# A two-layer decoder with a mixture-of-experts block: the order of the first loads, norms and projections

## The reference, cut to what matters

```python
mem_n = rms_norm(mem, mem_norm_g)               # 256 memory rows of 1024
h = rms_norm(x, g_mix_pre[0])                   # 512 tokens of 1024
proj = h @ w_in[0]                              # 1024 -> 1408 columns
q, k, v, qm = ...                               # 12 query heads, 3 key heads, 3 value heads, 4 memory-query heads
tok = mixer_a(q, k, v, attn_sink[0], cos_p, sin_p)   # rotary, banded attention of radius 128, with a sink
mkv = mem_n @ w_mem_kv[0]                       # 1024 -> 512: memory keys and values
mo = memory_attention(qm, km, vm)
o = jnp.concatenate([tok, mo], axis=-1) @ w_o[0]
```

## Time and profile before

| what | us |
|---|---|
| median of 3 runs | 2366.46 |
| lowest and highest run | 2361.76 and 2366.80 |
| the profiled execution, its own time | 2361.32 |
| its span | 2359.4 |
| PE busy in the span | 2047.8 (87%) |
| DVE busy | 1086.5 (46%) |
| ACT busy | 615.6 (26%) |

### The profile page before, as it was taken

One profiled execution on the slowest core, in us unless ns is written; L12 is line 12 of the kernel. 1 busy time (PEld: TensorE's weight loads), 2 busy tenths in 40 slices (PEclk: granted clock), 3 DMA queues, 4 the chain that ended last, 5 costly groups with the idle time before them and its releaser, 6 DMA issues. The chain is left out here.

```text
span 2359.4 us, 28557 instructions
## 1 busy us (share of the span) xinstructions
PE 2047.8 (87%) x11901; PEld 1430.9 (61%) x11901; DVE 1086.5 (46%) x2065; ACT 615.6 (26%) x1154; POOL 82.3 (3%) x103
## 2 busy tenths in 40 slices
PE   4977999999999899999999798878778999667772
PEld 2455478888864564788888686666455667322231
DVE  2058554446345774654463665563355344311113
ACT  1025322223121562322231333331143121000001
POOL 0000000000000000000000001110000000000001
PEclk8999999999999999999999898999889999688896
DMA  6120033232131200332331430000101235699994
GB/s 229 36 72 1 1 107 107 72 107 107 63 134 38 78 1 1 108 107 78 101 107 63 146 122 22 3 3 23 62 27 36 81 112 183 241 390 395 397 397 164
DMA packets 146770, 266.80 MB, mean 113 GB/s; under 512 B 6695, under 2 KB 69390, under 8 KB 146446
## 3 DMA queue, kind: packets, MB, share of 16 engines
q1 hardware_dynamic: 140302, 241.85, 29.3%
q0 software_dynamic: 3456, 12.58, 1.5%
q10 hardware_dynamic: 2880, 10.49, 1.1%
HBM read 250.22 MB, written 18.87 MB: 114 GB/s over the span
## 5 line engine op out<-in xcount | busy, mean ns | idle before, releaser
L237 PE MATMUL ps<-arena 64*64 64x64 f32 (+10 forms) x6136 | 870.9, 363 | 154.2 <-DMA arena<-in_moe_w_gu 55.1
L237 PEld LDWEIGHTS ps<-arena 64*64 64x64 f32 (+2 forms) x6136 | 461.3, 155 | 534.2 <-issue 392.0
L247 PE MATMUL ps<-arena 128*128 128x128 f32 (+2 forms) x1181 | 178.5, 301 | 95.5 <-DVE arena L354 27.8
L247 PEld LDWEIGHTS ps<-arena 128*128 128x128 f32 (+2 forms) x1181 | 144.4, 153 | 148.0 <-issue 65.7
L377 DVE TENSOR_SCALAR arena<-arena 128x1024 int32<-128x1024 int32 (+1 forms) x204 | 138.0, 677 | 144.1 <-PE ps L243 83.6
L241 PE MATMUL ps<-HTr,WH1r 128*128 128x512 f32 (+1 forms) x448 | 170.1, 380 | 1.2 <-ACT T16r L956 1.2
L241 PE MATMUL ps<-HTr,WH0r 128*128 128x512 f32 (+1 forms) x448 | 169.8, 379 | 1.2 <-ACT T16r L956 1.2
L384 ACT ACTIVATE WH0r<-arena 128x1024 fp32r<-128x1024 f32 x86 | 91.5, 1063 | 215.8 <-DVE slot2r L380 92.3
L243 PE MATMUL ps<-T16r,WH0r 128*128 128x512 f32 (+1 forms) x384 | 144.1, 375 | 0.0
L243 PE MATMUL ps<-T16r,WH1r 128*128 128x512 f32 (+1 forms) x384 | 143.9, 375 | 0.0
L384 ACT ACTIVATE WH1r<-arena 128x1024 fp32r<-128x1024 f32 x82 | 87.2, 1064 | 198.4 <-DVE slot0r L380 106.2
(11 more groups left out here) (363 smaller groups left out, 2834.5 us busy)
## 6 DMA issues: line engine op xcount, KB each, us to landing
arena<-in_moe_w_gu SPq DMA_DIRECT2D x32, 2048.0 KB, 18.4
arena<-in_w_gate_up SPq DMA_DIRECT2D x44, 1024.0 KB, 6.8
arena<-in_moe_w_down SPq DMA_DIRECT2D x32, 1024.0 KB, 14.7
arena<-in_w_down SPq DMA_DIRECT2D x8, 2048.0 KB, 7.8
arena<-in_w_in SPq DMA_DIRECT2D x7, 2048.0 KB, 11.1
arena<-in_w_in SPq DMA_DIRECT2D x9, 1024.0 KB, 5.4
arena<-in_w_o SPq DMA_DIRECT2D x4, 2048.0 KB, 7.8
y_scr<-arena ACTq DMA_DIRECT2D x16, 512.0 KB, 6.8
```

The lines of the kernel that those rows point to most:

```text
L237: return e.matmul(o, l, r, start=start, stop=stop, skip_group_check=True)
L247: return e.transpose(o, i, ident[0:n, 0:n])
```

## The change

SP's list begins with the four token tiles, each with a semaphore of its own, then the 128 columns of the constants that hold the identity, and the first two norm weights. Behind them stand the first chunk of columns, the memory rows, the memory's weights, the second chunk, the third chunk (now into T16), and last the rest of the constants, the other 15 norm weights and the small tables. PE transposes only the first 16 rows of GR at first; the whole table is transposed behind the last bank.

The norm of the token tiles comes first, and DVE scales tile i + 1 before it moves tile i out. PE makes the first chunk's bank for tile i as soon as that tile is out, with the transposes of tiles 2 and 3 between the banks. The memory's transposes stand between the first and the second chunk, its first bank between the second and the third, the first two quarters of its keys between banks of the third chunk, its second bank behind it, and the last two quarters in the attention, at the places of layer 1. The memory rows move to the region PB and the scratch of the token norm to XSC, so that T16 is free for weights.

```diff
...
-        d_const, d_mem, d_gain, d_x, d_small = [mark(n, queue, 16) for n in (
-            "const_in", "mem_in", "gains_in", "x_in", "small_in")]
+        d_const, d_mem, d_gain, d_small, d_first = [mark(n, queue, 16) for n in (
+            "const_in", "mem_in", "gains_in", "small_in", "ident_in")]
+        d_x = [mark(f"x{i}_in", queue, 16) for i in range(NT)]
...
-        T16J = QKVJ(1, 2)
+        T16J = [QKVJ(l, 2) for l in range(2)]
...
         def load(e, j):
-            if j == T16J:
-                e.wait_ge(*a_post["dn", 0, "x", 3])
+            if j in T16J:
+                if j == T16J[1]:
+                    e.wait_ge(*a_post["dn", 0, "x", 3])
                 e.dma_start(jobs[j][0][0](T16f), jobs[j][0][1]).then_inc(*d_t16.up(j))
                 return
...
+        MEMI, XSC = i4(PBf), i4(place("XSC", U0 + 9728, 4096))
         NORMS = dict(
-            mem=(lambda i: T16[:, i], 2, 1024, lambda i: T16[:, 2 + i], gcol("mem_norm_g"), MEMT),
-            x=(lambda i: X[:, i], 4, 1024, lambda i: T16[:, i], gcol("g_mix_pre", 0), HT),
+            mem=(lambda i: MEMI[:, i], 2, 1024, lambda i: MEMI[:, 2 + i], gcol("mem_norm_g"), MEMT),
+            x=(lambda i: X[:, i], 4, 1024, lambda i: XSC[:, i], gcol("g_mix_pre", 0), HT),
...
-        def v_norm_tile(e, tag, i):
+        def v_norm_scaled(e, tag, i):
             src, nt, D_, scr, g, dst = NORMS[tag]
             ms, rs = [a[:, i:i + 1] for a in NS[tag]]
             e.wait_ge(*a_norm[tag, i])
             e.tensor_scalar(ms, ms, eps6, None, ALU.add).then_inc(*v_norm.up(tag, "ms", i))
             e.wait_ge(*g_pow[tag, i])
             e.tensor_scalar(scr(i), src(i), rs, None, ALU.mult).then_inc(*v_norm.up(tag, "h", i))
+
+        def v_norm_turned(e, tag, i):
+            src, nt, D_, scr, g, dst = NORMS[tag]
             for k0 in range(0, D_ // P, 4):
                 n = min(4, D_ // P - k0)
                 iv = k4(held(tag, i, k0)[:, 0:n * P])
                 e.wait_ge(*p_norm[tag, i, k0])
                 e.tensor_tensor(dst[:, k0:k0 + n, i * P:(i + 1) * P], iv, g[:, k0:k0 + n].unsqueeze(2).broadcast_to((P, n, P)),
                                 ALU.mult).then_inc(*v_norm.up(tag, "out", i, k0))
+
+        def v_norm_tile(e, tag, i):
+            v_norm_scaled(e, tag, i)
+            v_norm_turned(e, tag, i)
+
+        def v_norm_tiles(e, tag):
+
+            for i in range(NORMS[tag][1] + 1):
+                if i < NORMS[tag][1]:
+                    v_norm_scaled(e, tag, i)
+                if i:
+                    v_norm_turned(e, tag, i - 1)
...
         def p_qkv_first(e):
-            for c in range(3):
-                loaded(e, QKVJ(0, c))
+
+            p_norm_tile(e, "x", 0)
+            p_norm_tile(e, "x", 1)
+            loaded(e, QKVJ(0, 0))
+            for i in range(NT):
+                e.wait_ge(*v_norm["x", "out", i, 4])
+                p_qkv_bank(e, 0, i, 0)
+                if i < 2:
+                    p_norm_tile(e, "x", i + 2)
+            for i in range(2):
+                p_norm_tile(e, "mem", i)
+            loaded(e, QKVJ(0, 1))
+            for i in range(NT):
+                p_qkv_bank(e, 0, i, 1)
+            e.wait_ge(*v_norm["mem", "out", 1, 4])
+            p_mkv_bank(e, 0, 0)
+            loaded(e, QKVJ(0, 2))
+            for i in range(NT):
+                p_qkv_bank(e, 0, i, 2)
+                if i % 2 == 0:
+                    p_mkv_turn(e, 0, 0, i // 2)
+            for c in range(2):
+                slot_done[QKVJ(0, c)] = (p_qkv, ("qkv", 0, 3, c))
+            p_mkv_bank(e, 0, 1)
+            slot_done[T16J[0]] = slot_done[MKV(0)]
+            e.wait_ge(*d_gain["all"])
+            tr(e, bank(e, "gains", v_norm, ("gains",))[:, 0:103], GR).then_inc(*p_norm.up("gains"))
+            for i in range(NT):
+                p_prepare(e, 0, 0, i)
...
+        def a_qkv_first(e):
+            for c in range(2):
+                for i in range(NT):
+                    if on_act(0, i, c):
+                        a_qkv_bank(e, 0, i, c)
+            a_mkv_bank(e, 0, 0)
+            for i in (0, 2):
+                a_qkv_bank(e, 0, i, 2)
+                a_mkv_turn(e, 0, 0, i // 2)
+            a_mkv_bank(e, 0, 1)
+            for i in range(NT):
+                a_prepare(e, 0, 0, i)
+
+        def v_qkv_first(e):
+            for i in range(2):
+                v_norm_scaled(e, "mem", i)
+            for c in range(2):
+                for i in range(NT):
+                    if not on_act(0, i, c):
+                        v_qkv_bank(e, 0, i, c)
                 if c == 0:
-                    e.wait_ge(*v_norm["x", "out", 3, 4])
-                for i in range(NT):
-                    p_qkv_bank(e, 0, i, c)
-                slot_done[QKVJ(0, c)] = (p_qkv, ("qkv", 0, 3, c))
-            for i in range(NT):
-                p_prepare(e, 0, 0, i)
+                    for i in range(2):
+                        v_norm_turned(e, "mem", i)
+            for i in (1, 3):
+                v_mkv_split(e, 0, 0, i // 2)
+                v_qkv_bank(e, 0, i, 2)
+            e.wait_ge(*d_const["all"])
+            v_rope_first(e)
+            e.wait_ge(*d_small["all"])
+            e.tensor_scalar(nsink, sink, -1.0, None, ALU.mult).then_inc(*v_qkv.up("nsink"))
+            e.wait_ge(*p_norm["gains"])
+            e.tensor_copy(GC[:, 16:103], held("gains")[:, 16:103]).then_inc(*v_norm.up("gains"))
+            e.wait_ge(*vec.last)
+            for i in range(NT):
+                v_prepare(e, 0, 0, i)
 
...
-            if l == 1 and n in MEM_AT:
-                memory(e, 1, *MEM_AT[n])
+            if n in MEM_AT:
+                memory(e, l, *MEM_AT[n])
...
         def sync(e):
-            e.dma_start(C, consts).then_inc(*d_const.up("all"))
-            e.dma_start(T16[:, 0:2, :], I["mem"][0].rearrange("(i p) d -> p i d", p=P)).then_inc(*d_mem.up("all"))
-            r0 = 0
+            for i in range(NT):
+                e.dma_start(X[:, i], I["x"][0, i * P:(i + 1) * P, :]).then_inc(*d_x[i].up("all"))
+            e.dma_start(C[:, 0:P], consts[:, 0:P]).then_inc(*d_first.up("ident"))
+            rows, r0 = [], 0
...
-                e.dma_start(GR[r0:r0 + n, :], v).then_inc(*d_gain.up("all"))
+                rows.append((GR[r0:r0 + n, :], v))
                 r0 += n
-            e.dma_start(X, I["x"][0].rearrange("(i p) d -> p i d", p=P)).then_inc(*d_x.up("all"))
-            for j in range(3):
-                load(e, j)
+            for dst, v in rows[:2]:
+                e.dma_start(dst, v).then_inc(*d_first.up("gains"))
+            load(e, QKVJ(0, 0))
+            e.dma_start(MEMI[:, 0:2, :], I["mem"][0].rearrange("(i p) d -> p i d", p=P)).then_inc(*d_mem.up("all"))
+            load(e, MKV(0))
+            load(e, QKVJ(0, 1))
+            load(e, QKVJ(0, 2))
+            e.dma_start(C[:, P:], consts[:, P:]).then_inc(*d_const.up("all"))
+            for dst, v in rows[2:]:
+                e.dma_start(dst, v).then_inc(*d_gain.up("all"))
...
             row(I["g_mix_post"][0], "mix", 0)
-            for j in range(3, len(jobs)):
+            for j in range(WOJ(0, 0), len(jobs)):
                 load(e, j)
...
         def tensor(e):
-            e.wait_ge(*d_const["all"])
-            e.wait_ge(*d_gain["all"])
-            tr(e, bank(e, "gc", v_norm, ("gc",))[:, 0:103], GR).then_inc(*p_norm.up("gc"))
-            for i in range(2):
-                p_norm_tile(e, "mem", i)
-            e.wait_ge(*v_norm["mem", "out", 1, 4])
-            for i in range(2):
-                p_mkv_bank(e, 0, i)
-            for i, hp in HALVES:
-                p_mkv_turn(e, 0, i, hp)
-            for i in range(NT):
-                p_norm_tile(e, "x", i)
+            e.wait_ge(*d_first["gains"])
+            tr(e, bank(e, "gc", v_norm, ("gc",))[:, 0:16], GR[0:16]).then_inc(*p_norm.up("gc"))
...
 
         def vector(e):
             e.wait_ge(*p_norm["gc"])
-            e.tensor_copy(GC, held("gc")[:, 0:103]).then_inc(*v_norm.up("gc"))
-            for i in range(2):
-                v_norm_tile(e, "mem", i)
-            for i, hp in HALVES:
-                v_mkv_split(e, 0, i, hp)
+            e.tensor_copy(GC[:, 0:16], held("gc")[:, 0:16]).then_inc(*v_norm.up("gc"))
+            v_norm_tiles(e, "x")
             for l in range(2):
                 if l == 0:
...
         def scalar(e):
+            for i in range(NT):
+                e.wait_ge(*d_x[i]["all"])
+                a_norm_tile(e, "x", i)
             e.wait_ge(*d_mem["all"])
             for i in range(2):
                 a_norm_tile(e, "mem", i)
-            for i in range(2):
-                a_mkv_bank(e, 0, i)
-            for i, hp in HALVES:
-                a_mkv_turn(e, 0, i, hp)
...
+            norm("x")
             norm("mem")
-            norm("x")
```

More of the change, by code:

```diff
@@ L302, in build @@
         slot_done = {}
-        T16J = QKVJ(1, 2)
+        T16J = [QKVJ(l, 2) for l in range(2)]
         def slot(j):
```

(48 more changed lines are left out.)

## The result

| | before | after |
|---|---|---|
| median of 4 runs each | 2365.45 | 2327.93 |
| lowest and highest | 2361.76 and 2366.80 | 2327.08 and 2336.30 |
| ratio of the runs, 95% interval | | 0.9851, 0.9833 to 0.9869 |
| the profiled execution | 2361.32 | 2336.30 |
| its span | 2359.4 | 2334.5 |

The change takes 37.5 us off the median. The profiled execution of the changed kernel is the slowest of its four, so its span shows only 24.9 us of that.

A forecast was written before the change was run, and what follows sets the result against it. PE sets the pace only from 64.12 to 142.57 us, otherwise waiting for loads and short chains. First split 32.9 earlier, less 1.2 in the attention, is 31.7 less: 2329.6 or 2334.8, so forecast 2332, range 2326 to 2340.

The forecast's parts named there:

- The start: Head of the kernel: norm weights land at 9.0 us; first bank starts at 15.3, bound by PE's own transposes.
- Rival 1: Head of the load queue is slow: tile loads or norm weights land late, 24.7 to 28.0 us less; chance 0.12.
- The first bank: First bank of the first chunk of columns: 9.8 us, against 6.87 for each later bank of 512 columns.
- Transposes between banks: Among PE's column banks: 1.2 us per tile, 2.4 for token tiles 2 and 3, 2.4 for the memory's two.
- The cover: Behind the third chunk: the memory's second bank hides DVE's rotary step with 3 us to spare; uncovered it costs 5.49.
- Rival 5: Before the attention: the memory's second bank does not cover the rotary step, so 5.5 us return; chance 0.03.
- The quarters in the attention: Layer 0's attention: two quarters of the memory's keys cost 0.3 us at unit 3 and 0.9 at unit 6, together 1.2.
- Rival 2: Layer 0's attention takes back more: the split-to-scores chain is not covered, 2.5 us instead of 1.2; chance 0.07.
- the sign of being wrong: Layer 0's attention: the prediction called itself wrong if the attention grows by over 2.5 us.
- rivals 3 and 4: Banks behind the first: clock falls once more, 2.9 us more, chance 0.04; or stays low, 51 us slower, chance 0.02.

The follow-up runs named there:

- one_x: The changed kernel with the tokens in one load of 2048 KB instead of four tile loads; 2323.76 us in one run.
- tile1_late: The changed kernel with only token tile 0 transposed ahead of the first bank, tile 1 behind it; 2336.74 us in one run.
- before_ahead: The kernel before, with only DVE's scaling of token tile i + 1 ahead of moving tile i out; 2356.33 us in one run.
- no_cover: The changed kernel with the memory's second bank directly behind its first, ahead of the third chunk; 2336.89 us in one run.
- again: The changed kernel once more, unedited, 5 runs; median 2325.3 us, ratio 0.9839 to the kernel before.
- quarters_in: The changed kernel with the last two quarters of the memory's keys behind the memory's second bank, none in layer 0's attention; 2325.67 us in one run.
- gains17: The changed kernel with all 17 norm weights loaded in front instead of two, PE waiting for them all; 2329.27 us in one run.

## Why the prediction was right, point by point

The time lies in the stated range (2326 to 2340), 4 us below the forecast of 2332. The mechanism was right; some terms of the sum were too large.

That the time fell into the range was in part luck. The gain was bounded at 26.7 to 33.9 us, and the 37.5 measured lie outside; taken from the median before, 2365.45, a gain of 33.9 would have given 2331.6. The range reaches lower because it also counts from the 2361.3 of the profiled execution, 4.1 us under that median. The bounds allowed for another start and another attention, but for nothing quicker between the first bank and PE's end, where 4.6 of the 5.3 us arose by which the first split came too early.

- **The start.** Norm weights at 9.15 (9.0 forecast), first bank at 14.72 (15.3), bound by PE's transposes as said. Rival 1 did not come: four tile loads cost no more than one load of the same bytes, within 0.6 us (`one_x`).
- **The first bank** was mis-sized: 9.8 forecast, 7.1 measured, 2.7 of the 5.3 us that the first split came too early. "I count that once: only the transposes of two tiles stand ahead of the first bank, as now" failed, since it is not "as now". Before, tile 3's eight stood alone behind a wait. Now 16 stand together, and the clock is up from the first product on (0.47 us from its record to the next, 1.01 in `tile1_late`). `tile1_late` gives the slow bank back (10.18). It is not certain in each execution: of eleven with 16 or more transposes ahead, ten had a first bank of 7.0 to 8.0 us and one of 9.6. All five first banks with eight behind a wait took 8.9 to 10.2 (two each in the traces of before and `before_ahead`, the memory's and the columns', and one in `tile1_late`).
- **Transposes between banks** were taken at 1.2 us per tile from four of 0.63; eight in a row between banks take 0.87 (21.62 to 22.50). Four tiles make 1.3 us and the two quarters 0.3. The rest of the 4.6 us by which bank start to PE end was shorter (93.7 against 98.3) is 0.2 of hand-over, since the 9.8 counts up to the bank's evacuation, and rounding; the banks behind the first took the 6.87 and 5.16 forecast.
- **The cover** of the rotary step: 3 us to spare forecast, 2.43 measured, worth 4.3 us (`no_cover`). Rival 5 did not come.
- **The quarters in the attention**: 0.3 and 0.9 forecast, 0.31 and 0.80 measured. Rival 2 did not come, nor did any wait follow behind unit 6 (in `again` DVE's lead never falls below 38.5 from there to the attention's end). The attention as a whole does not show this price: it was 2.5 us longer than before in the first trace, just short of the sign of being wrong, and 0.1 in `again`, at mean clocks of 0.92 and 0.98.
- **The clock between banks**: no bank behind the first was slow in any run, so rivals 3 and 4 fall.
- **From the split to the end** nothing was expected to change. That is nearly true of `again` (38.7 at the split, 35.9 at the end), while the profiled execution of the changed kernel lost 13 us behind the split at lowered clocks. Execution-to-execution spread is thus larger than most terms of this sum. Markers near the change, the first split above all, told kernels apart to a few tenths where medians of five runs left 2 to 5 us open, but only once the landing of the norm weights (8.59 to 9.86) and the length of the first bank were taken out.
- **What stays open.** Each alone, the overlap of the norm tiles was worth 6.9 us (`before_ahead`), the cover 4.3 (`no_cover`) and the place of the two quarters 3.8 (`quarters_in`), all at the first split. The rest of the 38 us, from the order of the loads and from the banks laid beside the norms, is argued from the rows; no run separates it.

## What to carry to other kernels

Order the first loads by who waits first, and put small tables that are wanted late behind the weights; here that, and matrix work with inputs at hand laid beside chains over several engines, took 38 us off the start. Keep a tile-wise chain one tile ahead of its consumer: it removes the hand-over, and it keeps PE's work together, which shows in the clock. Judge such an edit by a marker just behind it, and the total by medians.

## What the runs showed of the hardware

- Transposes alone were followed by the higher clock in `before_ahead`: 0.58 in 48 to 52, then 0.96 in 52 to 55, where PE had run nothing else since 48. The next eight ran at 0.50 again, behind a pause of 1.58 us.
- One kernel's first bank took 9.60 us in one execution and 7.13 in another. The Trainium skill ("TensorE: Matmul & The Clock Gate", section "What's actually happening") says that the number of slow products at a start varies from run to run of one kernel; these two executions agree.
- At the start of these traces the granted clock stands at 1.00 even where products take twice their time (0.85 us against 0.43 from one record to the next, 15.9 to 21 in `tile1_late`), so durations have to be read there.
- The same stretch of the same kernel costs 2.2 to 2.4 us more in some executions than in others: granted clock 0.80 near 915 in five traces, 0.86 to 1.00 in seven.
- The first loads do not land alike in each execution: the same norm weights behind the same loads came between 8.59 and 9.86.
- A load of 1 to 7 KB in a filled queue cost some 0.13 to 0.16 us (1.96 for 15 in `gains17`, 2.7 for 17 before).
